# Attention scores in quarters of TensorE's array, a level's scores with its left keys alone, and three changed orders on VectorE

## The reference, cut to what matters

```python
D_MODEL, SEQ, N_META, GLA_HEADS, GLA_DK, GLA_DV = 2048, 512, 16, 4, 256, 512
HEAD_DIM, N_Q_HEADS, N_KV_HEADS, GROUP, WINDOW, BLOCK = 64, 32, 8, 4, 128, 128

def gla_layer(x, s0, norm_w, w_in, w_gk2, b_gk2, onorm, w_out, chunk):
    proj = rmsnorm(x, norm_w) @ w_in
    q, k, v, gate, glr = jnp.split(proj, ...)
    g = log_sigmoid(glr @ w_gk2 + b_gk2) / GATE_LOGIT_NORM
    # b = cumsum(g); scores[i, j] = sum_d q[i,d] k[j,d] exp(b[i,d] - b[j,d]), j <= i
    o, S = gla_recurrence(q, k, v, g, s0, chunk)
    o = rmsnorm(o, onorm).reshape(B, L, GLA_VAL_DIM) * jax.nn.silu(gate)
    return x + o @ w_out, S

def window_mask(qpos, kpos):
    return (kpos >= 0) & (kpos <= qpos) & (qpos - kpos < WINDOW)

def swa_banded(q, k, v, sinks):      # a block of 128 queries, the block of keys before it and its own
    s = jnp.einsum('bnqhgd,bnkhd->bnhgqk', qb, kc) * (HEAD_DIM ** -0.5)
    s = jnp.where(mask[None, :, None, None], s, NEG_INF)
    p = sink_softmax(s, sinks)
    return jnp.einsum('bnhgqk,bnkhd->bnqhgd', p, vc)

def swa_layer(x, k, v, norm_w, w_in, sinks, w_out, attend):
    q, gate = jnp.split(rmsnorm(x, norm_w) @ w_in, [Q_WIDTH], axis=-1)
    o = attend(q, k, v, sinks)
    return x + (o * jax.nn.silu(gate)) @ w_out
```

## Time and profile before

| | us |
|---|---|
| median of 3 runs | 1797.02 (1796.41 to 1797.85) |
| the profiled execution's own time | 1800.52 |
| its span, first to last instruction | 1798.5 |
| TensorE busy | 1746.8 (97%) |
| VectorE busy | 1062.3 (59%) |
| ScalarE busy | 876.1 (49%) |
| GpSimd busy | 224.6 (12%) |

### The profile page before, as it was taken

The page is one execution under the profiler, slowest core; times in us unless marked ns, Lnnn a source line. Parts: engine busy times, 40 slices in busy tenths (PEclk is TensorE's granted clock), DMA queues, the critical chain, the costliest instruction groups (busy, mean ns, idle before and its releaser), DMA issues.

```text
span 1798.5 us, 36259 instructions
## 1 busy us (share of the span) xinstructions
PE 1746.8 (97%) x14273; PEld 1368.7 (76%) x14273; DVE 1062.3 (59%) x2268; ACT 876.1 (49%) x1343; POOL 224.6 (12%) x313
## 2 busy tenths in 40 slices
PE   6999999999999999999999999999999999989996
PEld 4788876787677867786677777777777877778885
DVE  6634646574557546864766874655665566564343
ACT  7545442553345444553345664544555455454442
POOL 1410010111011001101105103011000100011110
PEclk7999999999999999999999999999999999989998
DMA  9523322552255226542445443232233332234432
GB/s 304 152 72 95 83 53 87 170 167 77 59 173 168 71 65 184 194 139 74 137 156 177 158 113 103 77 82 82 70 82 82 82 86 70 72 89 134 110 99 100
DMA packets 270548, 204.49 MB, mean 114 GB/s; under 512 B 8116, under 2 KB 254080, under 8 KB 269136
## 3 DMA queue, kind: packets, MB, share of 16 engines
q1 hardware_dynamic: 251200, 131.71, 26.4%
q0 software_dynamic: 19232, 71.13, 11.7%
HBM read 168.05 MB, written 38.80 MB: 115 GB/s over the span
## 4 chain that ended last, share of the span: by engine, by line
PE 86%; DVE 8%; ACT 3%; issue 2%; DMA 1%; POOL 0%; SPq 0%; DVEq 0%; ACTq 0%; POOLq 0%
PE PP L604 56%; PE PP L852 8%; PE PP L633 3%; PE BS L696 2%; PE BS L507 2%; PE B L1045 2%; PE B L727 2%; PE BS L756 2%; PE B L507 1%; DVE W L1826 1%; PE BS L1002 1%; PE PP L1138 1%; PE B L778 1%; ACT W L1224 1%; PE BS L754 1%
## 5 line engine op out<-in xcount | busy, mean ns | idle before, releaser
L604 PE MATMUL PP<-H,W 128*128 128x280 f16 (+1 forms) x8640 | 1052.0, 281 | 1.0 <-ACT AR L1556 0.7
L604 PEld LDWEIGHTS PP<-H,W 128*128 128x128 f16 x8640 | 833.5, 98 | 187.5 <-issue 22.1
L1224 ACT ACTIVATE W<-W,SCL 128x1024 f16<-128x1024 f32 x240 | 262.5, 1138 | 311.2 <-DVE SCL L1757 270.2
L1826 DVE SCALAR_TENSOR_TENSOR W<-W,SCL 128x1024 f16<-128x1024 f32 x240 | 309.6, 1299 | 134.6 <-ACT W L1224 130.1
L1213 ACT ACTIVATE wjunk<-W 128x2048 bf16<-128x2048 f32 x120 | 227.7, 1897 | 13.9 <-DMA W<-in_w_out_a 10.7
L852 PE MATMUL PP<-O,W 128*128 128x280 f16 x1536 | 189.0, 283 | 2.2 <-DVE W L1826 1.2
L852 PEld LDWEIGHTS PP<-O,W 128*128 128x128 f16 x1536 | 147.5, 98 | 41.8 <-issue 7.1
L1597 ACT ACTIVATE AR<-AR 128x128 f32<-128x128 f32 x136 | 53.0, 391 | 86.6 <-DVE AR L2368 86.6
L604 PE MATMUL PP<-O,W 128*128 128x280 f16 x576 | 69.6, 282 | 0.5 <-DVE AR L2308 0.5
L2001 DVE SCALAR_TENSOR_TENSOR AR<-AR,B 128x512 f32<-128x512 f32 x32 | 23.9, 747 | 73.1 <-PE B L727 51.2
L2084 DVE SCALAR_TENSOR_TENSOR H<-PP,SCL,H 128x560 f32<-128x560 f32 x48 | 38.3, 799 | 46.5 <-PE PP L852 44.2
(11 more groups left out here) (349 smaller groups left out, 1877.3 us busy)
## 6 DMA issues: line engine op xcount, KB each, us to landing
W<-in_w_in_a SPq DMA_DIRECT2D x48, 1024.0 KB, 5.9
W<-in_w_in_b SPq DMA_DIRECT2D x32, 1024.0 KB, 6.1
out<-AR POOLq DMA_DIRECT2D x36, 512.0 KB, 4.5
AR<-in_state_gla POOLq DMA_DIRECT2D x32, 512.0 KB, 5.7
W<-in_w_out_b SPq DMA_DIRECT2D x16, 1024.0 KB, 6.0
W<-in_w_out_a SPq DMA_DIRECT2D x16, 512.0 KB, 5.3
W<-in_w_out_a SPq DMA_DIRECT2D x32, 256.0 KB, 3.8
W<-in_w_kv SPq DMA_DIRECT2D x8, 1024.0 KB, 5.9
```

The lines of the kernel that those rows point to most:

```text
L604: last = mm(PP[j % 2][:, c, 0:cols], w[:, k, :], x[:, c * cols:(c + 1) * cols], start=s_, stop=e)
L1224: A(w_parts(j % 2)[0][:, ks], W[:, j % 2, ks], ACT.Copy, scale=SCL[:, j % 4, 0:1]).then_inc(w_hi, 1)
L1826: STT(out=low[:, ks], in0=W[:, j % 2, ks], scalar=SCL[:, j % 4, 0:1], in1=high[:, ks], op0=ALU.mult, op1=ALU.subtract).then_inc(w_ready, 1)
```

## The change

- **Quadrant scores.** For tiles 1 to 3 each product of 128 queries with 256 keys becomes two of 64 queries with 192 keys: the first 64 queries with the previous block and the own block's first half, the last 64 with the previous block's second half and the own block. What is left out is what the mask `causal` replaces or what it never takes. Tile 0 is cut the same way. The row half of the array is the head's, the column half is the queries'.
- **Level 64.** The products of level 64 take only the 64 left keys of a tile as weights.
- **Last group.** Four instead of three batches are copied to `early`. They are then gated by feature tile, one gate of 512 columns for each of the two tiles (`tile_late`), the first ahead of the second projection's gate and the second behind it. ScalarE sums each tile's squares by itself. The weights of the following unit are scaled and their low halves made behind the masked copies of a batch and no longer ahead of them.
- **First head.** `low_rank_low` stands ahead of unit 3's scale and first low half.
- **Last head.** In quarters 3 to 6 and 16 to 19 the state update (and the norm) stands ahead of the output projection's addition.

```diff
         GS = sb("GS", [P, 3])
-        OS = sb("OS", [P, KV + 1])
+        OS = sb("OS", [P, KV + 2])
         out_fix = sb("out_fix", [P, 4])
...
         Qz = take([DB // 2, P])
-        early = take([3, 2 * P])
+        early = take([4, 2 * P])
         Pn, PnT = take([SMP]), take([P])
...
                 w = P if l == NL - 1 else P // 2
+                rows = P // 2 if l == 0 else P
                 for t in range(NT):
                     for kt in range(KT):
-                        last = mm(bank[:, t * w:(t + 1) * w], a[:, kt, COLS[t]], queries(kt, COLS[t]), start=(kt == 0),
-                                  stop=(kt == KT - 1))
+                        last = mm(bank[0:rows, t * w:(t + 1) * w], a[:, kt, t * P:t * P + rows], queries(kt, COLS[t]),
+                                  start=(kt == 0), stop=(kt == KT - 1))
                 x = l - (NL - NLX)
...
                         bank, c = (B0, B1)[r % 2], 2 * P * (r // 2)
-                        if k:
-                            last = mm(bank[:, c:c + 2 * P], q[:, COLS[k]], key[:, (k - 1) * P:(k + 1) * P], start=True, stop=True)
-                        else:
-                            mm(bank[:, c + P - META:c + P], q[:, COLS[0]], key[:, SEQ + SMP:TOK], start=True, stop=True)
-                            last = mm(bank[:, c + P:c + 2 * P], q[:, COLS[0]], key[:, COLS[0]], start=True, stop=True)
+                        for s in range(2):
+                            rows = slice(HD * s, HD * (s + 1))
+                            own, x = bank[rows], q[:, k * P + HD * s:k * P + HD * (s + 1)]
+                            if k:
+                                w = slice(c + HD * s, c + HD * s + P + HD)
+                                last = mm(own[:, w], x, key[:, (k - 1) * P + HD * s:k * P + HD * (s + 1)], start=True, stop=True)
+                            else:
+                                mm(own[:, c + P - META:c + P], x, key[:, SEQ + SMP:TOK], start=True, stop=True)
+                                last = mm(own[:, c + P:c + P + HD * (s + 1)], x, key[:, 0:HD * (s + 1)], start=True, stop=True)
                 else:
...
+                def tile_squares(j, at):
+                    act.wait_ge(late_done, j + 1)
+                    A(wjunk[:, 0:SEQ], O[:, 2 * i + j, 0:SEQ], ACT.Square, accum_out=OS[:, at:at + 1]).then_inc(o_summed, 1)
+
                 def squares(cols, at, gated):
...
                 if last:
-                    act.wait_ge(late_done, 1)
-                    squares(slice(0, SEQ), KV, (NT + GRP) * i + NT)
+                    tile_squares(0, KV)
                     act.wait_ge(o_summed, i + 1)
+                    tile_squares(1, KV + 1)
+                    act.wait_ge(o_summed, i + 2)
                     squares(slice(SEQ, LIVE), i, (NT + GRP) * (i + 1))
...
                         head_scores(i, n)
+                    if first(h) and n in (3, 4):
+                        (low_rank_scale, low_rank_low)[n - 3]()
                     if not (first(h) and n < 4):
...
                         prepare(2, 1)
-                    if first(h) and n in (3, 4):
-                        (low_rank_scale, low_rank_low)[n - 3]()
                     if n % 2:
...
                         scale(12)
+                    if 3 <= q < 7 or 16 <= q < 20:
+                        head_seqs(i, q, 0)
                     if q < 8 and q % 2:
...
                         outa_add(6 + q // 4, q % 4)
-                    head_seqs(i, q, 0)
+                    if not (3 <= q < 7 or 16 <= q < 20):
+                        head_seqs(i, q, 0)
                     if q % 4 in (1, 2) and q < 21:
...
+            def tile_late(i, j):
+
+                dve.wait_ge(gate_done, 4 * HEADS + 2 * i + j + 1)
+                dve.wait_ge(b_gated, (NT + GRP) * i + NT)
+                o = tile(O, 2 * i + j)[:, 0:SEQ].rearrange("p (k n) -> p k n", k=NT)
+                return STT(out=o, in0=early[:, :, j * P:(j + 1) * P], scalar=0.5, in1=o, op0=ALU.mult, op1=ALU.mult)
+
             def batch_gate(i, k):
...
                 spread_q(i)
-                stashed = 3 if last else 2
+                stashed = 4 if last else 2
                 for n in range(8):
...
                     if last and n == 6:
-                        batch_late(i, 0)
-                        batch_late(i, 1)
-                        batch_late(i, 2).then_inc(late_done, 1)
+                        tile_late(i, 0).then_inc(late_done, 1)
+                        unit_gate(i, 1)
+                        tile_late(i, 1).then_inc(late_done, 1)
                     if 1 <= n < NB + 1:
...
                         group_low(i, n // 2 + 1, n % 2)
-                    elif n in (0, 3):
-                        group_scale(i, n // 3 + 1)
-                        group_low(i, n // 3 + 1, 0)
-                    elif n in (1, 4):
-                        group_low(i, n // 3 + 1, 1)
+                    elif n == 0:
+                        group_scale(i, 1)
+                        group_low(i, 1, 0)
+                    elif n == 1:
+                        group_low(i, 1, 1)
                     elif n == 2:
...
                         batch_keep(i, n - 1)
+                    if last and n == 3:
+                        group_scale(i, 2)
+                    if last and n in (3, 4):
+                        group_low(i, 2, n - 3)
                     if not last and n in (1, 3):
...
                             batch_late(i, k)
-                    if last and n == 5:
-                        unit_gate(i, 1)
...
-            dve.wait_ge(o_summed, KV + 1)
+            dve.wait_ge(o_summed, KV + 2)
             V.tensor_reduce(out_fix[:, 0:1], OS[:], AX.X, ALU.add).then_inc(os_ready, 1)
```

## The result

| | median us | runs | ratio to before, 95% interval |
|---|---|---|---|
| before | 1797.28 (1795.10 to 1800.06) | 15 | |
| changed | 1791.63 (1789.20 to 1794.46) | 15 | 0.9968 (0.9961 to 0.9976) |

The kernel is 5.65 us faster. Forecast were 11.3, in a range that begins at 7.0: the sign was right, half of the gain is missing. The profiled execution of the changed kernel took 1791.63 us, 8.9 less than that of before. Single executions differ by several us, so the ledger is made by stages, and what the clock does in one of them is kept apart.

The account below looks back on a forecast made before the run. TensorE, busy for 97% of the span, was taken to bound the kernel. Terms 5.4 + 2.4 + 0 + 1.1 + 0 + 2.35 = 11.3 us, so 1797.0 - 11.3 = 1785.7 us; 8-in-10 range 1782.5 to 1790.0.

Parts of the forecast that it names:

- later batches, the blocks: Quadrant scores of tiles 1 to 3 in the attention groups: a block takes 0.805 us instead of 1.06, 21 x 0.255 = 5.4 us.
- first batches: Quadrant scores of tile 0 in the attention groups: about 0.85 us instead of 1.20, seven times 0.35, 2.4 us saved.
- new wait ahead of L534: Inner attention groups: VectorE and ScalarE taken as 2 us ahead of TensorE, so no new wait, 0 us.
- level 64, the three heads ahead of the last: Level 64 with left keys: some 0.7 us a head less on TensorE, swallowed by the wait behind level 32, 0 us.
- first head's order: Low-rank block at 74.07: TensorE's 1.10 us wait goes and is carried on, 1.1 us gained; ends 0.3 and 1.1.
- last head's order: Last state product: its 1.34 us wait moves to tile 19, some 1.3 us; sum 0, ends -0.5 and +1.3.
- last group: Last attention group: squares' reduction 2.0 us sooner plus 0.35 from the first scores, 2.35 us; ends 0.8 and 2.8.
- Rival 1: Inner groups' scores: column halves take turns or passes start in strict order; 1802.7 us, slower; 7%.
- Rival 2: Quadrant scores: weight loads into quarters don't hide, a block takes 0.97 us, 0.09 saved a batch; 1790.4 us; 8%.
- Four slots for eight products of a quarter: Later score blocks: all four array quarters work at once, 4 slots of 160 ns, 0.64 + 0.165 = 0.805 us.
- the prediction's working from it, 1.60 us: Later score blocks under strict program order: 9 slots, 1.44 + 0.165 = 1.60 us, a loss of 11 us in all; not adopted.
- The wait behind level 32 in the last head: TensorE's 1.20 us wait there was to grow by 0.6 us as level 64 got shorter, gaining 0 us.

## Why the prediction was off

Step by step, us gained (the measured ones from traces, each over its own stretch):

| step | forecast | measured |
|---|---|---|
| later batches, the blocks | 5.4 | 5.4 (0.255 each) |
| first batches | 2.4 | 2.1 (0.30 each) |
| new wait ahead of L534 | 0 | -2.4 (0.345 each) |
| level 64, the three heads ahead of the last | 0 | 0.0 |
| first head's order | 1.1 | 1.1 |
| last head's order | 0 | -1.3 (in three traces of four) |
| last group | 2.35 | 2.2 to the last sum (of it about 0.3 by the first scores) |
| sum | 11.3 | 7.1 |

The five parts alone add up, by their ratios, to 0.9966 where the changed kernel has 0.9968: they are additive within their intervals. In us that is 4.7, 2.3, 0.7, -0.2 and -1.4: 6.1. Between this and the 7.1 of the traces lie the intervals, the transfers in the last head, whose waits scatter from one execution to the next, and the drop of the clock behind the last group.

**The step that failed first** is the sentence "The trace has VectorE and ScalarE 2 us ahead, so nothing new waits." It came from one release in the group, the copy of the second weighted sum. In a group TensorE waits for the others at many places, and the one with the least cover decides. For L534 it was 0.3 us, readable in the profile of before, where the gate's second ScalarE row ends at 1206.43 and L534 stands at 1206.73:

```profile
1205.73 0.70 ACT L1286 ACTIVATE AR<-PP,SCL 128x544 f32<-128x544 f32 x1
```

Two blocks, 0.51 us, eat that, and in the changed kernel L534 starts 0.15 behind the release: 0.51 - 0.30 + 0.15 = 0.36. The term stood at 0 in the sum and measured -2.4. Rival 1 and 2, which were to catch a loss in the quadrants, looked at TensorE alone; the sign that the prediction named for a wrong forecast, gaps inside the inner groups, is the one that came.

**The second** is "Sum 0; ends a loss of 0.5 and a gain of 1.3" for the last head's order. Where the wait would go was right: tile 19, 1.41 us for 1.34. What came besides is the wait at 944. What the step left out is, as far as the traces go, the transfer: that a sooner update of the states is a sooner store, beside a weights' load that ScalarE needs. The order's place among VectorE's instructions was followed, the DMAs that it triggers weren't.

**What was right.** Four slots for eight products of a quarter: 0.81 us a block, 0.805 forecast. Of the block's 16 passes 4 have started by 1197.70 and 8 by 1197.91, TensorE in the windows 1197.66:1197.70 and 1197.87:1197.91:

```profile
1197.67 0.39 PE L1007 MATMUL BS<-AR 64*64 64x192 f32 x4
...
1197.67 0.56 PE L1007 MATMUL BS<-AR 64*64 64x192 f32 x8
```

Within a four the starts lie about 7 ns apart, and the last three fours start 0.16 us apart, the 160 ns that the forecast had for one pass. The Trainium skill (TensorE: Matmul & The Clock Gate, "The mechanism" in Part 3) says that matmuls keep the order of the program at their start and at their end. The records don't contradict it: their starts rise through the block, and so do their ends, as far as the profile models them. What they contradict is the prediction's working from it, 1.60 us, which took the two passes of one product to follow each other; the fours fit only if a quarter's next pass comes behind one pass of each of the other three. The block of before is alike, in pairs, so the prediction was wrong to read its 1.06 us against that page. Level 64's gain in the loop's heads went into the wait behind level 32, to 0.02 us. The first head's low part and the last group's chain up to the last sum came out within 0.2 us; how much of the latter reaches the output projection depends on the drop of the clock.

**What stays open.** The wait behind level 32 in the last head was to grow, and shrank from 1.20 to 0.73. VectorE's work there stands behind an addition that waits for the residual's transfer (2.23 us before; after:)

```profile
762.53 0.80 DVE L2094 SCALAR_TENSOR_TENSOR H<-PP,SCL,H 128x560 f32<-128x560 f32 x1 [1.21 <-DMA H<-x0T]
```

From the last product of level 32 to the next product it takes 0.36 to 1.59 us in the traces without the new level 64 and 0.77 to 1.55 in those with it, where no drop of the clock falls into it. The scatter of that transfer is larger than level 64's 0.56; what level 64 does there was not isolated. Nor is it known why the squares at 903 start 9.7 us behind the weights' issue in one execution and 11.9 in another, nor why one of the traces with the last head's new order has no wait at 944.

## To carry to other kernels

A stage in which the bounding engine is 100% busy hides how near the others are: before shortening it, list every release it takes there with its cover (release's end against the use), and take the smallest, not a typical one. When an order is changed, follow the DMAs that the moved instructions release as well; with the DMA engines about 80 to 90% busy, a store 0.7 us sooner went, in three traces of four, with weights used 1.0 to 1.2 later. Where a product can be moved out of a wait, one input tile's delay can be enough.

## What the runs showed of the hardware

Products that use one quarter of TensorE's array each (64 rows, 64 columns) run four at a time: 16 passes of 192 float32 columns in 0.81 us with the block's end, where one after the other, at the 0.16 us between two passes of one quarter, they would need 2.6.

The clock's drops are not the same in two executions of one program. Half rate held for 13.7 to 20.5 us within the first 44 us in the fourteen profiles, and for 3.4 to 10.2 at the end of the attention. In seven of the fourteen another drop of 3.41 us stood at 768 to 772 (three), 907 (one) or 1102 to 1105 (three), each behind a stretch in which TensorE had waited or done transposes, which the traces without such a drop have as well; the one in the changed kernel cost 1.4 us for 24 products. That is the size of the effects looked for here, so two profiled executions can't be subtracted as wholes.
